# Order of the recurrence, first loads and bias product, and addresses of three operands, in a one-core transformer kernel

## What is computed

```
y, u = split(hn @ w_in)                       # 1024 channels each
y  = gelu(y)
uc = conv_b + sum over 4 taps of u_pad[t + tap] * conv_w[tap]
r  = sigmoid(uc @ wa + ba)                    # wa, wx: 4 blocks of 256 x 256
ig = sigmoid(uc @ wx + bx)
log_a = -8 * r * softplus(-lam);  a = exp(log_a)
b_in = sqrt(-expm1(2 * log_a)) * (ig * uc)
hs_t = a_t * hs_(t-1) + b_in_t                # over the 256 tokens
out = (hs * y) @ w_out
```

## Time and profile before

| | |
|---|---|
| median of 3 runs | 1187.43 us (1184.91 to 1190.97) |
| profiled execution | 1186.28 us, span 1185.0 us |
| TensorE (PE) busy | 1142.9 us, 96% of the span |
| VectorE (DVE), ScalarE (ACT), GpSimd (POOL) busy | 669.1, 585.6 and 296.6 us |
| mean granted TensorE clock | 0.986 of full speed |
| DMA | 207.89 MB, mean 175 GB/s |

### The profile page before, as it was taken

One profiled execution on the slowest core, in us unless ns is written; L12 is line 12 of the kernel. 1 busy time (PEld: TensorE's weight loads), 2 busy tenths in 40 slices (PEclk: granted clock), 3 DMA queues, 4 the chain that ended last, 5 costly groups with the idle time before them and its releaser, 6 DMA issues.

```text
span 1185.0 us, 19539 instructions
## 1 busy us (share of the span) xinstructions
PE 1142.9 (96%) x8221; PEld 1061.8 (90%) x8221; DVE 669.1 (56%) x1039; ACT 585.6 (49%) x893; POOL 296.6 (25%) x187
## 2 busy tenths in 40 slices
PE   7999999999999999999899999999999769999997
PEld 5999989999979999889898789999889768999986
DVE  5654765577666454337897566344247686543324
ACT  6555555455536544337533445444344874544432
POOL 1022100000004444512321105444500101544440
PEclk9999999999999999999999999999999889999999
DMA  8569474544646666555443447665656334765560
GB/s 247 188 210 335 142 240 133 178 142 144 190 149 193 198 181 200 198 168 177 131 147 111 132 143 230 186 189 193 197 164 192 101 114 158 222 188 183 191 195 36
DMA packets 158209, 207.89 MB, mean 175 GB/s; under 512 B 13551, under 2 KB 131497, under 8 KB 158122
## 3 DMA queue, kind: packets, MB, share of 16 engines
q1 hardware_dynamic: 154650, 193.69, 52.1%
q0 software_dynamic: 3472, 12.95, 3.4%
HBM read 205.53 MB, written 4.24 MB: 177 GB/s over the span
## 4 chain that ended last, share of the span: by engine, by line
PE 91%; DVE 3%; ACT 3%; SPq 1%; issue 1%; DMA 1%; POOL 0%; ACTq 0%; DVEq 0%
PE bank L490 19%; PE bank L493 18%; PE bank L496 18%; PE bank L507 10%; PE bank L513 10%; PE bank L510 10%; PE bank L850 2%; DVE wlo L1346 1%; PE bank L776 1%; ACT whi L951 1%; PE bank L786 1%; PE bank L798 1%; DMA ring<-in_c_onehot 1%; PE bank L553 1%; SPq L2101 0%
## 5 line engine op out<-in xcount | busy, mean ns | idle before, releaser
L1346 DVE TENSOR_TENSOR wlo<-raw,whi 128x1024 fp32r<-128x1024 f32 (+1 forms) x281 | 346.9, 1263 | 231.5 <-ACT whi L951 230.6
L951 ACT ACTIVATE whi<-raw 128x1024 fp32r<-128x1024 f32 x368 | 365.2, 1042 | 117.3 <-PE bank L513 111.9
L490 PE MATMUL bank<-hh,whi 128*128 128x256 f32 x1792 | 288.1, 282 | 1.7 <-ACT hh L983 1.7
L1904 POOL TENSOR_TENSOR wlo<-raw,whi 128x1024 fp32r<-128x1024 f32 x87 | 223.2, 2565 | 256.3 <-ACT whi L951 256.2
L493 PE MATMUL bank<-hh,wlo 128*128 128x256 f32 x1792 | 283.4, 279 | 0.0
L496 PE MATMUL bank<-hl,whi 128*128 128x256 f32 x1792 | 283.0, 279 | 0.0
L490 PEld LDWEIGHTS bank<-hh,whi 128*128 128x128 f32 x1792 | 243.6, 188 | 7.0 <-issue 5.7
L493 PEld LDWEIGHTS bank<-hh,wlo 128*128 128x128 f32 x1792 | 242.4, 188 | 0.0
L496 PEld LDWEIGHTS bank<-hl,whi 128*128 128x128 f32 x1792 | 242.0, 188 | 0.0
L1911 POOL TENSOR_TENSOR st<-st,half 128x1 f32<-128x1 f32 x18 | 10.3, 579 | 389.6 <-DVE st L1363 360.8
L507 PE MATMUL bank<-whi,gh 128*128 128x512 f32 x264 | 81.5, 390 | 0.0
(11 more groups left out here) (292 smaller groups left out, 1184.8 us busy)
## 6 DMA issues: line engine op xcount, KB each, us to landing
raw<-in_ffn_w_in SPq DMA_DIRECT2D x88, 512.0 KB, 3.7
raw<-in_w_in SPq DMA_DIRECT2D x72, 512.0 KB, 4.7
raw<-in_ffn_w_out SPq DMA_DIRECT2D x44, 512.0 KB, 3.3
raw<-in_hgrn_w_in SPq DMA_DIRECT2D x32, 512.0 KB, 4.3
raw<-in_w_ffn_gate SPq DMA_DIRECT2D x22, 512.0 KB, 4.5
raw<-in_w_ffn_up SPq DMA_DIRECT2D x22, 512.0 KB, 4.1
raw<-in_w_ffn_down SPq DMA_DIRECT2D x22, 512.0 KB, 3.3
raw<-in_w_branch SPq DMA_DIRECT2D x16, 512.0 KB, 4.4
```

The lines of the kernel that those rows point to most:

```text
L490: T.matmul(out, wh[:, i, c], xh[:, k, :], start=first and (i, k) == pairs[0], stop=False)
L951: A.activation(half_of(whi, j, h), half_of(raw, j, h), ACT.Copy).then_inc(s_hi[j % NS][h], 1)
L1346: V.tensor_tensor(half_of(wlo, j, h), half_of(raw, j, h), half_of(whi, j, h).bitcast(f32), ALU.subtract).then_inc(s_lo[j % NS][h], 1)
L1904: G.tensor_tensor(half_of(wlo, j, 1), half_of(raw, j, 1), half_of(whi, j, 1).bitcast(f32), ALU.subtract).then_inc(s_lo[j % NS][1], 1)
```

## The change

It has six parts:

- The norm row is issued ahead of x on SP.
- The eight column loads move from SP to GpSimd's queue, behind its second power, and raise a semaphore of their own (`s_cols`). The bias product and its evacuation go behind the unit xbc 1 and wait for the other eight small loads.
- `eh` and `el`, which take the inputs of wo and ho, are laid over `hh` and `hl`, 64 bytes lower. Counted from `whi` they start a multiple of 512 bytes on; `hh` starts 64 bytes past one.
- A gap of 416 bytes moves `ch` and `cl` from 96 bytes past a multiple of 512 to one (and with them the layer's later buffers).
- In the recurrent layer the gate units come ahead of ly 0 and ly 1, and the steps of ScalarE and VectorE get another order, with tangents and decays in separate loops.
- `gated_input` moves from GpSimd to VectorE.

The diff, cut to these:

```diff
+        shifted = ExitStack()
+        eh = sbuf(shifted, "eh", [128, 8, 256], f32r)
+        el = sbuf(shifted, "el", [128, 8, 256], f32r)
+        shifted.close()
...
         hh = sbuf(root, "hh", [128, 8, 256], f32r)
...
+        sbuf(lr, "gap_ch", [128, 104])
         ch = sbuf(lr, "ch", [128, 8, 256], f32r)
...
+        lru_gate_unit(0)
         cols(("ly", 0), lw, 0, 256)
-        lru_gate_unit(0)
+        lru_gate_unit(1)
         cols(("ly", 1), lw, 256, 256)
-        lru_gate_unit(1)
         cols(("ly", 2), lw, 512, 256)
         cols(("ly", 3), lw, 768, 256)
...
-            tq.wait_ge(s_small, 256)
+            tq.wait_ge(s_cols, 128)
...
             T.transpose(banks[6][:, 0:120], vrows, ident[0:120, 0:120]).then_inc(s_full[6], 1)
-            turn(("u",), 7)
-            tq.wait_ge(*free(("u",)))
-            T.matmul(banks[7][0:16, 0:384], rb[:, 0:16], rb[:, 16:400], start=True, stop=True).then_inc(s_full[7], 1)
             for j in range(1, 4):
                 project_columns(("xbc", j), 0)
+                if j == 1:
+                    turn(("u",), 7)
+                    tq.wait_ge(s_small, 128)
+                    tq.wait_ge(*free(("u",)))
+                    T.matmul(banks[7][0:16, 0:384], rb[:, 0:16], rb[:, 16:400], start=True, stop=True).then_inc(s_full[7], 1)
...
-            add_product(("wo",), 4, hh, hl, *of_norm(1), 2)
+            add_product(("wo",), 4, eh, el, *of_norm(1), 2)
...
+            lru_gates(0)
             project_columns(("ly", 0), 6)
-            lru_gates(0)
+            lru_gates(1)
...
-            lru_gates(1)
...
+                    aq.wait_ge(*evac("vec"))
+                if j == 1:
...
-                    aq.wait_ge(*evac("vec"))
...
-                A.activation(hh[:, sl, :], acc[:, sl, :], ACT.Copy, scale=0.5).then_inc(s_hh, 1)
+                A.activation(eh[:, sl, :], acc[:, sl, :], ACT.Copy, scale=0.5).then_inc(s_hh, 1)
...
-            def conv_unit(j):
-                conv_start(j)
-                conv_round(j)
-
             def lru_gates(h):
-                use(("lg", h))
...
+
+            def tangents(h):
...
-                    A.activation(aT[:, c, :], rg[:, c, :], ACT.Exp, scale=vec[:, 96 + c:97 + c])
-                    A.activation(th[:, c, :], rg[:, c, :], ACT.Tanh, scale=vec[:, 120 + c:121 + c]).then_inc(s_aa, 1)
+                    A.activation(th[:, c, :], rg[:, c, :], ACT.Tanh, scale=vec[:, 120 + c:121 + c])
+
+            def decays(h):
+                for c in range(4 * h, 4 * h + 4):
+                    A.activation(aT[:, c, :], rg[:, c, :], ACT.Exp, scale=vec[:, 96 + c:97 + c]).then_inc(s_aa, 1)
             def root_of(n):
...
             def gated(n):
-                gelu(n)
...
             project_pair([("lu", 0), ("lu", 1)], 6, bc_lr, [lambda: None, lambda: None])
+            conv_start(0)
             use(("lu", 2))
-            conv_unit(0)
+            conv_start(1)
+            conv_round(0)
+            conv_start(2)
+            conv_round(1)
             use(("lu", 3))
-            conv_unit(1)
+            conv_start(3)
+            conv_round(2)
+            use(("lg", 0))
+            lru_gates(0)
+            conv_round(3)
             use(("ly", 0))
-            lru_gates(0)
-            conv_unit(2)
-            conv_unit(3)
+            tangents(0)
+            use(("lg", 1))
+            lru_gates(1)
+            tangents(1)
             use(("ly", 1))
-            lru_gates(1)
-            use(("ly", 2))
+            decays(0)
+            decays(1)
             for n in range(4):
                 root_of(n)
+            use(("ly", 2))
+            gelu(0)
+            gelu(1)
+            gated(0)
+            gelu(2)
+            gated(1)
             use(("ly", 3))
-            for n in range(4):
-                gated(n)
+            gelu(3)
+            gated(2)
+            gated(3)
             add_product(("lo",), 4, 7)
...
             def conv_unit(j):
-                sl = slice(2 * j, 2 * j + 2)
...
                     conv_taps(uc[:, c, :], up, c, 40, 8 + c + 1)
+
+            def conv_rest(j):
+                sl = slice(2 * j, 2 * j + 2)
...
+
+            def gated_input(n):
+                sl = slice(2 * n, 2 * n + 2)
+                vq.wait_ge(*evac("lg", 0, n))
+                V.tensor_tensor(ig[:, sl, :], ig[:, sl, :], uc[:, sl, :], ALU.mult).then_inc(s_ti, 1)
             def input_factor(n):
...
             project_pair([("lu", 0), ("lu", 1)], 6, [lambda: u_of(0), lambda: u_of(1)])
+            conv_unit(0)
             use(("lu", 2))
+            conv_unit(1)
+            conv_rest(0)
             u_of(2)
-            conv_unit(0)
+            conv_rest(1)
             use(("lu", 3))
+            conv_unit(2)
             u_of(3)
-            conv_unit(1)
+            conv_rest(2)
+            use(("lg", 0))
+            conv_unit(3)
+            conv_rest(3)
             use(("ly", 0))
+            gated_input(0)
+            gated_input(1)
             y_of(0)
-            use(("lg", 0))
-            conv_unit(2)
-            conv_unit(3)
+            use(("lg", 1))
+            use(("ly", 1))
+            gated_input(2)
+            gated_input(3)
             input_factor(0)
             input_factor(1)
-            use(("ly", 1))
             y_of(1)
-            use(("lg", 1))
             input_factor(2)
             input_factor(3)
+            scan(0)
+            scan(1)
             use(("ly", 2))
             y_of(2)
-            scan(0)
-            scan(1)
+            gated(0)
+            scan(2)
+            gated(1)
             use(("ly", 3))
+            scan(3)
             y_of(3)
-            scan(2)
-            gated(0)
-            gated(1)
-            scan(3)
             gated(2)
             gated(3)
             add_product(("lo",), 4, 7)
...
                 power(factor(0, t), ("n", 0, t)).then_inc(s_pow, 1)
+            at_row = 0
+            for name in ("conv_w", "conv_b", "lru_conv_w_2", "lru_conv_b_2", "lru_ba_2", "lru_bx_2", "lru_lambda_2"):
+                src = a[name][0]
+                src = src.rearrange("k (c p) -> (k c) p", p=128) if len(src.shape) == 2 else src.rearrange("(c p) -> c p", p=128)
+                G.dma_start(vrows[at_row:at_row + src.shape[0], :], src).then_inc(s_cols, 16)
+                at_row += src.shape[0]
+            G.dma_start(vrows[104:120, :], a["hgrn_lb_2"].rearrange("k (c p) -> (k c) p", p=128)).then_inc(s_cols, 16)
             split_to(0)
...
-            def gated_input(h):
-                for n in (2 * h, 2 * h + 1):
-                    sl = slice(2 * n, 2 * n + 2)
-                    gq.wait_ge(*evac("lg", 0, n))
-                    gq.wait_ge(s_ucl, n + 1)
-                    G.tensor_tensor(ig[:, sl, :], ig[:, sl, :], uc[:, sl, :], ALU.mult).then_inc(s_ti, 1)
-
-            use(("lg", 0))
-            gated_input(0)
-            use(("lg", 1))
-            gated_input(1)
             use(("ly", 3))
             add_product(("lo",), 4, 7)
...
+            S.dma_start(wrow[0:1, 0, :], rows[0].rearrange("(o n) -> o n", o=1)).then_inc(s_row[2], 16)
             S.dma_start(x[:, 0, :], a["x"][0, 0:128, :]).then_inc(s_x[0], 16)
             S.dma_start(x[:, 1, :], a["x"][0, 128:256, :]).then_inc(s_x[1], 16)
-            S.dma_start(wrow[0:1, 0, :], rows[0].rearrange("(o n) -> o n", o=1)).then_inc(s_row[2], 16)
...
-            at_row = 0
-            for name in ("conv_w", "conv_b", "lru_conv_w_2", "lru_conv_b_2", "lru_ba_2", "lru_bx_2", "lru_lambda_2"):
-                src = a[name][0]
-                src = src.rearrange("k (c p) -> (k c) p", p=128) if len(src.shape) == 2 else src.rearrange("(c p) -> c p", p=128)
-                S.dma_start(vrows[at_row:at_row + src.shape[0], :], src).then_inc(s_small, 16)
-                at_row += src.shape[0]
-            S.dma_start(vrows[104:120, :], a["hgrn_lb_2"].rearrange("k (c p) -> (k c) p", p=128)).then_inc(s_small, 16)
```

14 lines of the change are left out of this document (7 added, 7 removed).

## The result

The changed kernel takes 1178.96 us (median of 6 runs, 1177.46 to 1181.58), the kernel before beside it 1190.18 (6 runs): a ratio of 0.9912, with a 95% interval from 0.9891 to 0.9932, so 8 to 13 us less. The forecast was 1175.0 against a profiled 1186.28, a ratio of 0.9905. The two profiled executions differ by less: 1177.87 us (span 1176.6) against 1186.28 (span 1185.0). In the four later comparisons the kernel before has medians of 1188.67, 1190.26, 1188.63 and 1191.40 (70 runs, 1189.67 over all), so its profiled execution was one of the quicker ones. The number alone does not tell the forecast from two of its rivals, late columns (1179.5) and a recurrence that gains nothing (1179.0), which lie nearer to the measured median; the traces have to.

What follows compares the result with a forecast made beforehand. TensorE, with 91% of the chain, bounds the kernel through its waits and the half clock behind them. Start 5.8, recurrence 4.0, addresses 1.3 and 0.2 sum to 11.3 us: 1186.28 becomes 1175.0, range 1170.5 to 1181.0.

Steps and rivals of the forecast that it cites:

- late columns: Rival at the start: column loads land at 21.0, PE still waits 3.0 us; about 1179.5 us, chance 0.12.
- a recurrence that gains nothing: Rival in the recurrent stage: waits only move and 4 us more of them eat the gain; 1179.0 us, chance 0.10.
- The start, row ahead of x: Kernel start: norm row issued first, so the first unit ends at 18.0 instead of 19.0; gain 1.0 us.
- The columns: Bias columns' transpose: last column lands at 16.7, before PE asks at 18.0, so the wait goes; gain 3.0 us.
- a PE wait for the area tile near 18: Sign that the forecast is wrong: at the start PE still waits for the bias columns.
- the columns come only when VectorE's splits end: Start, by the skill's "DVE blocks DMA" box: POOL cannot write descriptors while VectorE has the shared pair; no size given.
- The clock behind that wait: From 22.00 to 27.00, behind the columns' wait: without it these 5.0 us of PE work take 3.2; gain 1.8 us.
- The recurrence: Recurrent stage and lo: VectorE's new order brings the last cl at 971.2 instead of 974.8; gain 4.0, walk 2.3 to 4.6.
- the worst case of the walk: Inside lo: half clock behind the wait for the third unit lasts through both parts; first half ends at 981.0, not 978.7.
- The 7 us of standing before lo: Ahead of lo: sign that the forecast is right, PE standing about 7 us there.
- The addresses: wo, ho and lo: six 512-column matmuls take 1.36 instead of 1.40 us; gain 1.3 in wo and ho, 0.2 in lo.
- The collision: Rival in wo, ho and lo: operands a multiple of 512 bytes apart make 288 matmuls dearer; up to 1242, chance 0.03.

Runs made afterwards that it cites:

- b_row: Kernel before with only the norm row issued ahead of x; ratio 0.9996 (0.9976 to 1.0015).
- best: Changed kernel with column loads ahead of GpSimd's powers, 16-column matmuls spread, and more reordering of recurrence and lo; 1174.25 us, ratio 0.9902 to the kernel before.
- a_off: Changed kernel with inputs of wo and ho 32 bytes past a multiple of 512 and the recurrence's rounded buffers 256 past; ratio 0.9923 to the kernel before.
- b_cols: Kernel before with only the column loads on GpSimd's queue and the bias product behind unit xbc 1; ratio 0.9956 (0.9939 to 0.9973).
- b_rec: Kernel before with only the recurrence's new order, the table's gate units and the gated input on VectorE; ratio 0.9964 (0.9946 to 0.9982).
- a_mix: Changed kernel with the 48 matmuls of 16 columns spread two by two between the 24 following 512-column ones; ratio 0.9905 to the kernel before.
- b_addr: Kernel before with only the new addresses: lower inputs of wo and ho, gap ahead of the recurrence's rounded buffers; ratio 0.9992 (0.9976 to 1.0009).
- a_gpool: Changed kernel with the gated input back on GpSimd, the rest of the new order kept; ratio 0.9936 to the kernel before.
- a_hh0: Changed kernel with the norm's rounded inputs 64 bytes lower too, a multiple of 512 bytes from the weights; ratio 1.0 to the kernel before.
- ctl: Changed kernel measured and profiled once more, no edit; 1178.24 us, ratio 0.9904 to the kernel before.
- r_rec: Changed kernel with roundings ahead of next conv starts, last y unit's split ahead of tangents, lo's third unit split earlier; 1174.21 us, ratio 0.9867 to the kernel before.
- p1: Changed kernel with the norm's rounded inputs 256 bytes past, bh 64 bytes further, the recurrence's rounded buffers 32 past; ratio 1.0021 to the kernel before.

## Why the prediction was right

The measured median lies 4 us above the forecast, inside the stated range and half a microsecond outside the narrower one (1172 to 1178.5) that was the forecast's own. Step by step:

- **The start, row ahead of x** (1.0): the first weight unit ended 0.76 us earlier, at 18.23; full clock came at 13.7 in this execution. In the nine other profiles with the row first it ended at 17.7 to 18.0, 1.0 to 1.3 earlier. By b_row everything is lost again unless the columns land early, as the walk had it in one sum with them.
- **The columns** (3.0): 2.06. The step that was mis-sized is the landing. I took 3.9 us from issue to landing, the median of the row loads, with 1.8 as the low end (which belongs to a store of that queue, `u_scratch<-ring`, not to a load). The last column took 7.1. None of the eight column loads took under 4.7 in any profile, and the last took 6.6 to 7.6 in eight of ten, 5.0 and 5.1 in the two without a wait (best, a_off). Of the eight other profiles with these loads behind the powers one shows no wait for them and seven 0.6 to 2.1 us. The late edge that I kept for the range had 7.2 and was the nearer one. The issues themselves (0.50 to 0.68 us) were right. So the sign "a PE wait for the area tile near 18" came, and the rival of late columns came true by a third: a wait, but none with a half clock behind it. That the columns come only when VectorE's splits end, which the prediction set beside this rival, did not happen: in a_off the last had landed at 17.3, while VectorE's four splits ran without a pause from 15.3 to 19.9. What makes the last load slow stays open.
- **The clock behind that wait** (1.8): b_cols, which shortens this wait to 0.62, has 1.5 us less between transpose and 16-column matmuls, and so has b_rec, where the load landed earlier and no half clock followed; so this term held, for executions that have the half clock. Another 0.4 us came from still groups at 113 ns behind the moved product, which no step foresaw.
- **What the prediction did not have: the half clock at the 16-column matmuls.** It begins 2.6 to 5.6 us behind the first of them in all twelve profiles with the 48 in a row, in that of before too, and lasts 3 to 10 us by chance. A wait is not the only thing behind which the clock falls. The records show TensorE busy throughout the 48. a_mix and best show the cause: the same matmuls, spread, and no fall in either. What it is about them that brings the half clock stays open.
- **The recurrence** (4.0, bounds 2.3 to 4.6): 2.46, 2.0 by the second profile. The walk of VectorE was right to 0.2 us: measured from u's first matmul, the last cl came at 971.1 on before's scale (walk 971.2), the first at 958.2 (958.3), lo's third unit at 971.4 (971.5). The gate waits were 1.05, 1.16 and 2.30 (1.3, 1.2, 2.8). What failed is the choice between the bounds, 2.3 with half clock through both parts behind the second wait and 4.6 with none: I took 4.0, above their middle. The half clock came behind that wait in all eight profiles of the new order that have it, and in the changed kernel lo's first half ended at 981.0 on before's scale, which is the worst case of the walk to 0.1 us. The worst case was the case. The 7 us of standing before lo were 5.3 and 6.8.
- **The addresses** (1.3 and 0.2): 0.56 and 0.51 in wo and ho, and the pace exactly 1.36. In lo the new pace reaches every matmul at full clock. The page SBUF — State Buffer of the Trainium skill, section SBUF: two separate sides, says that TensorE waits on nobody on the engine side; b_addr and a_off show a pace that changes with 32 bytes of distance, so the measurement decides against that reading, though only by 7 ns a matmul. Against the same page's port rule nothing speaks: the taps of a_gpool beside GpSimd's product took two to three times their time (1.42 and 2.00 us instead of 0.48 and 1.00) and TensorE's pace stayed.
- **The collision** (0.03) did not come in the changed kernel. a_hh0 shows that it exists in another place: at distance 0 the products with still weights do get dearer, by 2.3 ns, and there are 5376 of them. As a rival it had the right sign and the wrong group of instructions.

The sum came out right in part by luck. The terms of the profiled pair add up to 8.4 us, 2.9 under the forecast: the forecast had 1.2 too much for the row and the columns, 1.7 for the recurrence and lo, and did not have the 1.6 lost at the 16-column matmuls, against 1.8 gained in layer 1 and ahead of wo, which is not shown to be the change's. The ratio of the medians, 10.5 us with an interval of 8 to 13, holds both 8.4 and 11.3. The four single parts, each against the kernel before, give 0.5, 5.2, 1.0 and 4.3 us by their ratios, 10.9 together.

## What to carry to other kernels

Ask of the clock not only behind waits: here a run of 48 matmuls of 16 columns brought half clock as well, in a stretch that looks fully busy, and spreading them between long ones took it away. Spreading them shortened that stretch, though no gain of the whole kernel was shown for it alone. Where a walk of the engines gives a wait on TensorE like those seen here, count half clock behind it as the case to expect and not as the worst one (behind the 3.1 us wait of layer 1 it came in 12 of 14 profiles, behind a 2.3 us wait at the gates in 5 of 9, behind the 1.9 to 2.1 us for the columns in none of 5), and compare two profiles of one kernel before a difference of 1 to 2 us is put down to an edit. An address that is best for one form of a product can be the worst for another, so move the buffer of that form alone, as this change did.

## What the runs showed of the hardware

- Matmuls of 512 columns with the activations stationary: 227 ns at a distance of 0 or 256 bytes (modulo 512) between the two operands, 233 at 32, 64 and 96.
- Matmuls of 256 columns with the weights stationary: 120 ns at 0 and at 256, 117.8 at 64. They also run at 113 ns for whole units, at the same addresses: in the first block in all profiles with `hh` at 64 bytes; after the bias product in three (after, ctl, r_rec) and not in a_gpool, a_off, b_cols, a_mix and best; in layer 1 of block 2 in before, after and best, and not in ctl, another execution of the program of after. What selects between 113 and 117.8 stays open. The gates' products, whose order is another, took 120 ns with `ch` at 96, at 0 and at 256, and 117 to 118 at 32 (p1).
- The last of eight small loads (4 to 16 KB) of GpSimd's queue landed 6.9 and 7.1 us after its issue (b_cols, after), the first of them 5.1 and 5.0, where one small store of that queue took 1.8 at another time (before); with the loads ahead of the powers, in best, all took 4.7 to 5.2 and TensorE no longer waited for them.
